# Gates of the side input taken tile by tile, and tokens kept in column order to the last store

## The chip, the cores and the metric

The kernel runs on one core of one Trainium2 chip. The metric is the device time of one execution in microseconds (us); lower is better. Engines are named as in the profile: PE (TensorE matmul), PEld (its weight loads), DVE (VectorE), ACT (ScalarE), POOL (GpSimd) and SP (SyncE). The transfers that SP and ACT issue are on their queues (SPq, ACTq).

## The reference, cut to what matters

Four layers over x of 512 tokens by 1024 features, all in float32: sparse attention (nsa), differential attention (diff), neighbourhood attention on a grid of 8 rows by 64 columns (na) and attention from latents with rotary positions (mla). The last two are each followed by a gated side input p ("ple"):

```python
for i in range(DEPTH):
    xn = rmsnorm_2(x, norm_g[i])
    y = mixer_na(...) if i % 2 == 0 else mixer_mla(...)   # ends in (o * silu(z)) @ w_out
    h = x + y
    gate = jax.nn.sigmoid(rmsnorm_2(h, ple_norm[i]) @ ple_w_gate[i])
    x = h + gate * (p[i] @ ple_w_proj[i])
return rmsnorm_2(x, final_norm)
```

In na a token (r, c) of the grid, number 64 r + c, attends to all 8 rows and a window of 16 columns. Every other operation of the second half is either by token or, in mla, over all tokens alike, except for the rotary tables, which depend on a token's position.

## The kernel before

**Numbers and tiles.** A product of two float32 matrices is made of three matmuls on parts: each operand is split into a high part of reduced precision and the rest (low), and low x high, high x low and high x high are summed in PSUM (`products`, L367 to L395; the matmul is L393). Tokens are 4 tiles of 128. A projection of 512 output columns ("block") over 1024 features is 8 chunks of 128, and its weights are two units of 1 MB, a=0 and a=1, each 128 x 2048 elements.

**Weights.** SP loads units in order (L308) into a ring of three slots. The unit n may be loaded once the unit before it in its slot is used up (`consumed`, L297): its last matmul for a=0 (`w_used`), or the last bank of the block for a=1 (`bank_done`). ACT then writes the high part (`split_high`, L339), POOL the low part by subtraction (`split_low`, L348, in one instruction or in quarters), and PE waits for `w_ready`. Each engine's order is written out by hand: all waits are on semaphores, and an engine that waits holds all that is behind it.

**Order of products.** `project_tensor` goes a=0 for the four tiles, then a=1 for the four tiles, so the four banks are done one after the other in the last quarter of the block. `project_by_tile` (L655) does a=0 and a=1 for one tile before it goes to the next, on block 1. `project_turning` (L641) takes an order of (a, tile, tile to turn): `TWO_TO_TURN` and `INTERLEAVED` (L638, L639).

**A norm chain.** Between two layers x (in SBUF) is squared tile by tile on ACT (`square_x`, L682), POOL takes the root (`root_x`, L733 and L735), DVE scales (`norm_tile`, L777), PE transposes the tile (`turn_tile`, L633, 8 transposes), ACT copies the high part (`high_tile`, L688) and DVE subtracts the low part (`low_tile`, L783). A tile's turn needs its norm, and for tiles 2 and 3 also the low part of the tile two before; the next layer's product for a tile needs that tile's low part.

**na and mla attention** (`pair_tensor`, `pair_vector`, `pair_scalar` L1310, `pair_pool` L1369). 32 steps for 16 groups of two steps (2 heads, 256 queries). A step: scores on PE, mask and maximum on DVE (L1267), exponent on ACT (L825), division on POOL (`normalise`, L1377), transposes on PE (L1197), high part on ACT (L1320), low part on DVE (L1280), values on PE (L1216). A group ends in a sum (ACT L1326, DVE L1287) and `gate_out` on POOL: times silu(z), which lies in the place of x (L1384), high part (L1390), low part (L1394). Before, na is computed in column order (8 c + r) and `by_token` writes its result back to token order with a stride of 64 elements. x itself lies in DRAM (`x_scratch`) during an attention: ACT stores it before, and fetches it after group 16 of the attention (`load_x`, L700, four transfers), before it fetches p (L1725). The out projection starts inside the attention (`first_output`); its second unit is split at the loop's end by ACT (step `steps + LAG - 1`) and by POOL (step `steps + LAG + 2`, ahead of the last `gate_out`).

**After the attention** the residual stage (`residual_*`) adds y to x (L601), and PE turns the normed tiles: tile 0 inside the last product of the out projection, tiles 1 to 3 inside the 8 products of the side input (`ple_tensor`, L1711). Then come the gates (`gate_tensor` L1799, `gate_scalar` L1804 with the sigmoid L1812, `gate_vector` L1843 with L1849 and L1852, `gate_pool` L1876), which add gate * side input to x. For ple0 the norm chain of mla runs at their end, with the first turn in the last product of the block; the other three turns are in `mla_cq`, by `INTERLEAVED`. Then follow `mla_ckv`, `mla_rope` (banks 0 and 1, taken by DVE at L1976 and L1977) and `mla_z`. For ple1 the final norm and the store (L328, one transfer per tile) end the program.

## Time and profile before

| | |
|---|---|
| median of 3 runs | 1449.52 us (1446.53 to 1450.22) |
| profiled execution | 1441.95 us, span 1440.1 us, granted clock 0.995 |
| PE / DVE / ACT / POOL busy | 1359.3 / 615.1 / 717.2 / 774.3 us |
| na attention | about 884 to 965 us of the span |
| na_out, side input, gates of ple0 | 965 to 1060 us |
| mla_cq, mla_ckv, mla_rope | 1060 to 1110 us |
| mla attention | about 1220 to 1335 us |
| mla_out, side input, gates of ple1, last norm | 1335 to 1440 us |

Times inside the span count from its start. A row of the timeline has the start, the duration, the engine, the line, what it writes and reads, the number of like instructions merged, and in brackets how long the engine sat idle before it and what released it. A matmul's duration is longer than the distance to the next one, since matmuls are pipelined: 186 of them fill 42.0 us, 0.226 us each.

### The profile page before, as it was taken

Reading aid. Unit: us, or ns where it says so; the run is one execution under the profiler, and the core shown is the slowest. Engines: PE = TensorE matmul, PEld = TensorE weight load, DVE = VectorE, ACT = ScalarE, POOL = GpSimd, SP = SyncE. Lnnn points to the kernel's source line nnn. Section 1 sums busy time; section 2 is a strip of 40 time slices with the busy share of each in tenths; the row PEclk is TensorE's granted clock in tenths of the full one; section 3 lists DMA queues with packets and bytes.
Section 4 is the critical chain, followed back from the end, with each engine's and each line's share of the span. In section 5 each row is a group of like instructions: output and inputs, shape, how many; then the busy total and the mean of one; then the engine's idle time right before and its main releaser. Section 6 shows DMA issues by size and latency. Waiting matters only on the chain.

```text
span 1440.1 us, 20940 instructions
## 1 busy us (share of the span) xinstructions
PE 1359.3 (94%) x7818; PEld 1113.8 (77%) x7818; DVE 615.1 (43%) x1606; ACT 717.2 (50%) x1533; POOL 774.3 (54%) x729
## 2 busy tenths in 40 slices
PE   5999999999999999889999999889999998999997
PEld 4887877777878888667788887678778886778785
DVE  3322068887330011883510014943242045887133
ACT  4244268887332323774423326954443254887252
POOL 5355256776444434486535334986446334566652
PEclk9999999999999999999999999999999999999998
DMA  6233210100453231213344224333234221001521
GB/s 243 88 118 117 89 59 31 31 30 12 151 176 117 88 110 67 74 46 122 119 140 146 88 89 146 118 112 138 103 115 163 88 91 56 1 2 67 182 88 59
DMA packets 27876, 139.57 MB, mean 97 GB/s; under 512 B 3328, under 2 KB 3712, under 8 KB 16128
## 3 DMA queue, kind: packets, MB, share of 16 engines
q1 hardware_dynamic: 14112, 98.57, 19.2%
q10 hardware_dynamic: 13664, 39.66, 8.1%
q8 instruction: 63, 1.03, 0.3%
q14 instruction: 37, 0.30, 0.1%
HBM read 129.83 MB, written 8.39 MB: 96 GB/s over the span
## 4 chain that ended last, share of the span: by engine, by line
PE 73%; POOL 10%; DVE 9%; ACT 4%; issue 2%; DMA 1%; ACTq 0%; POOLq 0%; SPq 0%; DVEq 0%
PE psum L393 59%; PE psum L1169 3%; POOL w_free L1377 3%; PE psum L1216 3%; PE psum L1197 3%; POOL w_lo L348 3%; DVE w_free L1267 2%; PE psum L908 2%; POOL split L1394 1%; DVE arena L777 1%; PE psum L1182 1%; ACT w_hi L339 1%; DVE u_lo L1280 1%; DMA w_raw<-in_weights 1%; POOL split L1390 1%
## 5 line engine op out<-in xcount | busy, mean ns | idle before, releaser
L348 POOL TENSOR_TENSOR w_lo<-w_raw,w_hi 128x2048 fp32r<-128x2048 f32 (+2 forms) x118 | 424.2, 3608 | 409.4 <-ACT w_hi L339 400.0
L393 PE MATMUL psum<-u_lo,w_hi 128*128 128x512 f32 (+1 forms) x712 | 279.8, 393 | 0.9 <-DVE arena L1976 0.9
L393 PE MATMUL psum<-u_hi,w_lo 128*128 128x512 f32 (+1 forms) x712 | 277.3, 389 | 0.0
L393 PE MATMUL psum<-u_hi,w_hi 128*128 128x512 f32 (+1 forms) x712 | 277.3, 389 | 0.0
L339 ACT ACTIVATE w_hi<-w_raw 128x2048 fp32r<-128x2048 f32 (+1 forms) x93 | 172.9, 1859 | 120.5 <-DMA w_raw<-in_weights 101.7
L393 PE MATMUL psum<-w_hi,split 128*128 128x512 f32 x608 | 195.6, 394 | 3.6 <-POOL w_lo L348 2.1
L825 ACT ACTIVATE w_free<-w_free,neg_max 128x256 f32<-128x256 f32 (+3 forms) x320 | 183.6, 580 | 12.4 <-DVE neg_max L947 7.3
L393 PEld LDWEIGHTS psum<-u_lo,w_hi 128*128 128x128 f32 (+1 forms) x712 | 133.2, 187 | 30.4 <-POOL w_lo L348 1.3
L393 PEld LDWEIGHTS psum<-u_hi,w_hi 128*128 128x128 f32 (+1 forms) x712 | 133.1, 187 | 28.6
L393 PEld LDWEIGHTS psum<-u_hi,w_lo 128*128 128x128 f32 (+1 forms) x712 | 133.2, 187 | 27.5
L393 PE MATMUL psum<-w_hi,u_lo 128*128 128x512 f32 (+2 forms) x352 | 133.8, 380 | 5.2 <-DVE u_lo L783 2.8
L1280 DVE TENSOR_TENSOR u_lo<-psum,u_hi 128x512 fp32r<-128x512 f32 (+3 forms) x256 | 124.8, 520 | 31.0 <-ACT u_hi L1320 27.7
L393 PEld LDWEIGHTS psum<-w_hi,split 128*128 128x128 f32 x608 | 114.2, 188 | 29.0 <-POOL w_lo L348 3.0
L1320 ACT ACTIVATE u_hi<-psum 128x512 fp32r<-128x512 f32 (+3 forms) x256 | 109.3, 463 | 49.0 <-PE psum L1197 45.5
L393 PE MATMUL psum<-w_lo,u_hi 128*128 128x512 f32 (+2 forms) x352 | 132.1, 375 | 0.0
L393 PE MATMUL psum<-w_hi,u_hi 128*128 128x512 f32 (+2 forms) x352 | 132.1, 375 | 0.0
L1197 PE MATMUL psum<-ident,w_free 128*128 128x128 f32 x704 | 111.8, 283 | 21.0 <-POOL w_free L1377 15.5
L393 PE MATMUL psum<-w_lo,split 128*128 128x512 f32 x304 | 118.4, 389 | 0.0
L1197 PEld LDWEIGHTS psum<-ident,w_free 128*128 128x128 f32 x704 | 75.9, 141 | 51.6 <-POOL w_free L1377 31.3
L1377 POOL TENSOR_SCALAR w_free<-w_free,inv 128x256 f32<-128x256 f32 (+1 forms) x128 | 73.2, 586 | 64.5 <-DVE inv L1273 64.2
L1216 PE MATMUL psum<-u_lo,split 128*128 128x256 f32 (+1 forms) x416 | 102.9, 284 | 0.0
L520 DVE SCALAR_TENSOR_TENSOR split<-psum,split 128x512 fp32r<-128x512 f32 x40 | 27.6, 692 | 171.2 <-ACT split L512 157.2
(193 smaller groups left out, 2157.1 us busy)
## 6 DMA issues: line engine op xcount, KB each, us to landing
w_raw<-in_weights SPq DMA_DIRECT2D x90, 1024.0 KB, 4.8
x<-x_scratch ACTq DMA_DIRECT2D x12, 512.0 KB, 6.1
gain<-in_gains ACTq DMA_DIRECT2D x10, 512.0 KB, 4.4
gain<-in_strips ACTq DMA_DIRECT2D x16, 256.0 KB, 2.9
spare<-in_strips ACTq DMA_DIRECT2D x16, 256.0 KB, 2.9
x_scratch<-x ACTq DMA_DIRECT2D x16, 256.0 KB, 5.1
gain<-in_near ACTq DMA_DIRECT2D x8, 512.0 KB, 4.2
w_raw<-in_near ACTq DMA_DIRECT2D x8, 512.0 KB, 3.7
```

Source lines behind the costliest of these rows:

```text
L339: high = nc.scalar.activation(w_hi[b][:, c], w_raw[b][:, c], ACT.Copy)
L348: low = nc.gpsimd.tensor_tensor(w_lo[b][:, c], w_raw[b][:, c], w_hi[b][:, c].bitcast(F32), ALU.subtract)
L393: mm = nc.tensor.matmul(dst, lhs, rhs, start=(a == 0 and k == 0 and (wl, ul) == (0, 1)), stop=(a + 1 == u and k + 1 == nk and (wl, ul) == ...
L825: nc.scalar.activation(p_map(f, i, m, n), p_map(f, i, m, n), ACT.Exp, scale=-1.0, bias=stat_of(neg_max, i, m), accum_out=stat_of(row_sum, ...
L908: mm = nc.tensor.matmul(head_bank(d, r), buf[:, pt:pt + P], split[:, a + v:a + v + P], start=(kt == 0 and nth == 0), stop=(kt == kts[-1] a ...
L1169: mm = nc.tensor.matmul(score_place(f, i, m), *products[m][nth], start=(nth == 0), stop=(nth == 2 and f is not mla_flow))
L1197: tr = nc.tensor.transpose(psum[:, 4 + m, kt * P:(kt + 1) * P], p_map(f, i, m, n)[:, kt * P:(kt + 1) * P], ident[:])
L1216: mm = nc.tensor.matmul(dst, value_place(f, d, m, kt), pt_pair(buf, d, m, a, b), start=(br == 0 and m == 0 and kt == order[0] and nth == 0 ...
L1267: nc.vector.tensor_tensor_reduce(out=p_map(f, i, m, n), in0=score_bank(i, m, n), in1=bias_of(f, i, m), scale=-1.0, scalar=BIG, op0=ALU.add ...
L1280: nc.vector.tensor_tensor(u_lo[:, c], bank(4 + m, n), u_hi[:, c].bitcast(F32), ALU.subtract).then_inc(f.low, 1)
L1320: nc.scalar.activation(u_hi[:, pt_cols(i, m, n)], bank(4 + m, n), ACT.Copy).then_inc(f.high, 1)
L1377: nc.gpsimd.tensor_scalar(p_map(f, i, m, n), p_map(f, i, m, n), stat_of(inv, i, m), factor_of(f, i, m), ALU.mult, ALU.mult).then_inc(f.p, 1)
```

## The change

- The gates' second block goes tile by tile (`project_by_tile`), with the turns of mla's tiles 0 and 1 inside tiles 2 and 3 of it; `mla_cq` has the other two (`TWO_TO_TURN`). ACT, DVE and POOL follow in a new order: the split of unit (1,1) of the gates comes earlier on ACT, those of `mla_cq` later on POOL and its second one later on ACT.
- The turns of the residual stage are all inside the side input's products, none in the out projection.
- `mla_rope` uses banks 4 and 5, and DVE gives the four banks of `mla_z` free in advance.
- From na on, x stays in column order: the store to `x_scratch` is four contiguous transfers in place of eight strided ones, `gate_out` writes without the large stride, p and the rotary tables are laid out in column order on the host, and the last store puts the rows in their place.
- x is fetched during the na and mla attentions, tile by tile (tiles 0, 1, 2 at ACT's steps 18, 26, 34), and only tile 3 after it.
- In na, ACT splits the out projection's second unit two steps earlier, and POOL does it in quarters after groups 12 and 13 in place of one instruction after group 14; the last `normalise` comes ahead of group 12.

```diff
@@ -325,7 +325,8 @@
                 sp.wait_ge(chain_normed, final_chain.n + t + 1)
-                sp.dma_start(out[t * P:(t + 1) * P, :], at(final_chain.xn + t * D, D)).then_inc(out_written, 16)
+                tile = bass.AP(out.tensor, 16 * t * D, [[D, 16], [GRID_W * D, 8], [1, D]])
+                sp.dma_start(tile, at(final_chain.xn + t * D, D)).then_inc(out_written, 16)
             sp.wait_ge(out_written, 16 * NT)
@@ -695,8 +696,8 @@
-        def load_x(act, source):
-            for t in range(NT):
+        def load_x(act, source, tiles=range(NT)):
+            for t in tiles:
                 act.dma_start(x[:, t * D:(t + 1) * D], source[t * P:(t + 1) * P]).then_inc(x_back, 16)
@@ -1342,29 +1343,27 @@
                     high(i - LAG)
-                if f in (na_flow, mla_flow) and i == f.steps + LAG - 1:
+                if i == (f.steps if f is na_flow else f.steps + LAG - 1) and f is not nsa_flow:
                     split_high(act, RUNS[f.name + "_out"]["unit"] + 1)
+                if f is not nsa_flow and i >= 18 and i % 8 == 2:
+                    t = (i - 18) // 8
+                    act.wait_ge(f.gated, 4 * t + 4)
+                    load_x(act, x_scratch, (t,))
                 j = i - LAG - 4 - 2 * (B - 1)
...
-        def by_token(part, u, h, n):
-            o = split[:, part + u * T:part + (u + 1) * T].rearrange("p (r c) -> p c r", r=8)
-            if h == 1:
-                return o[:, 24:56, :]
-            if n == 1:
-                return o[:, 8:24, :]
-            at_ = split[:, part + u * T:part + u * T + 1]
-            return bass.AP(at_.tensor, at_.offset, [at_.ap[0], [56, 2], [1, 8], [GRID_W, 8]])
+        def in_columns(part, u, h, n):
+            o = split[:, part + u * T:part + (u + 1) * T]
+            edge, _ = rotated(o)
+            return o[:, 192:448] if h == 1 else o[:, 64:192] if n == 1 else edge
...
             if g % 2 == 1:
-                return o.rearrange("p (c r) -> p c r", r=8)
-            if n == 1:
-                return o[:, P:2 * P].rearrange("p (c r) -> p c r", r=8)
-            return o[:, 0:P].rearrange("p (s c r) -> p s c r", s=2, c=8)
+                return o
+            return o[:, P:2 * P] if n == 1 else o[:, 0:P].rearrange("p (s c) -> p s c", s=2)
@@ -1395,13 +1394,18 @@
             for i in range(2, f.steps + LAG + 5):
-                if i - 2 < f.steps:
+                if i - 2 < f.steps - (1 if f is na_flow else 0):
                     normalise(i - 2)
-                if f in (na_flow, mla_flow) and i == f.steps + LAG + 2:
-                    split_low(pool, RUNS[f.name + "_out"]["unit"] + 1)
+                if f is na_flow and i == f.steps:
+                    normalise(f.steps - 1)
+                if f is mla_flow and i == f.steps + LAG + 2:
+                    split_low(pool, RUNS["mla_out"]["unit"] + 1)
                 j = i - LAG - 5 - 2 * (B - 1)
...
                     gate_out(j // (2 * B))
+                if f is na_flow and i in (f.steps, f.steps + 2):
+                    for part in range(i - f.steps, i - f.steps + 2):
+                        split_low(pool, RUNS["na_out"]["unit"] + 1, part)
@@ -1712,7 +1716,7 @@
             pe.wait_ge(p_lo, nth + 1)
-            turning = {(0, 0): 1, (0, 2): 2, (1, 0): 3}
+            turning = {(0, 0): 0, (0, 1): 1, (0, 3): 2, (1, 1): 3}
             for i in range(2):
@@ -1799,7 +1803,7 @@
             project_tensor(pe, name, only=(0,))
-            project_tensor(pe, name, only=(1,), between=chain and {(1, 1, 3): lambda: turn_tile(pe, chain, 0)})
+            project_by_tile(pe, name, None, {(0, 2): lambda: turn_tile(pe, chain, 0), (0, 3): lambda: turn_tile(pe, chain, 1)} if chain else {})
@@ -1812,32 +1816,29 @@
             split_next(act, name, 0, 0)
-            for j in range(NT):
+            take(0, 0)
+            split_next(act, name, 0, 1)
+            for j in range(1, NT):
                 take(0, j)
-            split_next(act, name, 0, 1)
+            take(1, 0)
             if c is final_chain:
-                take(1, 0)
-                take(1, 1)
                 square_x(act, c, 0)
-                take(1, 2)
-                square_x(act, c, 1)
-                take(1, 3)
-                square_x(act, c, 2)
-                square_x(act, c, 3)
+                for j in range(1, NT):
+                    take(1, j)
+                    square_x(act, c, j)
                 return
             split_next(act, name, 1, 0)
-            take(1, 0)
+            square_x(act, c, 0)
             take(1, 1)
-            square_x(act, c, 0)
+            high_tile(act, c, 0)
+            square_x(act, c, 1)
             take(1, 2)
-            square_x(act, c, 1)
-            high_tile(act, c, 0)
+            high_tile(act, c, 1)
+            square_x(act, c, 2)
             take(1, 3)
+            high_tile(act, c, 2)
+            square_x(act, c, 3)
             split_next(act, name, 1, 1)
-            square_x(act, c, 2)
-            high_tile(act, c, 1)
-            square_x(act, c, 3)
-            high_tile(act, c, 2)
             high_tile(act, c, 3)
@@ -1855,23 +1856,14 @@
             take(1, 0)
-            take(1, 1)
             norm_tile(dve, c, 0)
-            take(1, 2)
-            if c is final_chain:
-                norm_tile(dve, c, 1)
-                take(1, 3)
-                norm_tile(dve, c, 2)
-                norm_tile(dve, c, 3)
-                return
-            low_tile(dve, c, 0)
-            norm_tile(dve, c, 1)
-            take(1, 3)
-            low_tile(dve, c, 1)
-            norm_tile(dve, c, 2)
-            norm_tile(dve, c, 3)
-            low_tile(dve, c, 2)
-            low_tile(dve, c, 3)
+            for j in range(1, NT):
+                take(1, j)
+                if c is not final_chain:
+                    low_tile(dve, c, j - 1)
+                norm_tile(dve, c, j)
+            if c is not final_chain:
+                low_tile(dve, c, 3)
@@ -1882,16 +1874,17 @@
                 return
-            for part in range(4):
-                split_low(pool, n + 2, part)
             root_x(pool, c, 0)
+            pool.wait_ge(chain_normed, c.n + 1)
+            split_low(pool, n + 2, 0)
+            split_low(pool, n + 2, 1)
             root_x(pool, c, 1)
-            split_low(pool, n + 3, 0)
-            split_low(pool, n + 3, 1)
+            pool.wait_ge(chain_normed, c.n + 2)
+            split_low(pool, n + 2, 2)
+            split_low(pool, n + 2, 3)
             root_x(pool, c, 2)
             root_x(pool, c, 3)
-            split_low(pool, n + 3, 2)
-            split_low(pool, n + 3, 3)
+            split_low(pool, n + 3)
@@ -1969,15 +1962,13 @@
+            dve.wait_ge(bank_free["dve"], 4 + RUNS["mla_rope"]["taken"])
+            dve.sem_inc(bank_free["dve"], 4)
             dve.wait_ge(rope_in, 16)
-            def take(i, j):
-                if j == 0:
-                    return nc.vector.tensor_tensor(at(ROPE_TMP), bank(0), COS, ALU.mult)
-                return nc.vector.tensor_tensor(at(QT), bank(1), SIN, ALU.mult)
-            project_vector(dve, "mla_rope", take, banks=2)
-            run = RUNS["mla_rope"]
-            dve.wait_ge(bank_free["dve"], 4 + run["taken"] + 4)
+            dve.wait_ge(bank_done, 4 * RUNS["mla_rope"]["block"] + 4)
+            done("dve", nc.vector.tensor_tensor(at(ROPE_TMP), bank(4), COS, ALU.mult))
+            done("dve", nc.vector.tensor_tensor(at(QT), bank(5), SIN, ALU.mult))
+            settle("dve", dve)
             done("dve", nc.vector.tensor_tensor(at(QT), at(QT), at(ROPE_TMP), ALU.add))
@@ -2067,13 +2058,12 @@
             project_tensor(pe, "na_out", gated_by=na_flow, only=(0,), begun=True)
-            project_tensor(pe, "na_out", gated_by=na_flow, only=(1,),
-                           between={(1, 1, 3): lambda: turn_tile(pe, ple_chains[0], 0)})
+            project_tensor(pe, "na_out", gated_by=na_flow, only=(1,))
             ple_tensor(pe, ple_chains[0], 0)
             gate_tensor(pe, ple_chains[0], "ple0_gate", mla_chain)
-            project_turning(pe, mla_chain, "mla_cq", INTERLEAVED)
+            project_turning(pe, mla_chain, "mla_cq", TWO_TO_TURN)
             project_tensor(pe, "mla_ckv")
-            project_tensor(pe, "mla_rope", banks=2)
+            project_tensor(pe, "mla_rope", banks=2, base=4)
             project_tensor(pe, "mla_z", only=(0,))
@@ -2147,15 +2136,12 @@
             chain_scalar(act, na_chain, "diff_out", x_scratch)
-            for r in range(8):
-                column = x[r:P:8, :].rearrange("c (t d) -> c t d", t=NT)
-                act.dma_start(bass.AP(x_scratch.tensor, r * GRID_W * D, [[D, 16], [16 * D, NT], [1, D]]), column)\
-                    .then_inc(x_spilled, 16)
+            for t in range(NT):
+                act.dma_start(x_scratch[t * P:(t + 1) * P], x[:, t * D:(t + 1) * D]).then_inc(x_spilled, 16)
             project_scalar(act, "na_v", split_heads_act(by_head), halves=True)
...
             load_strips(act, na_flow, 0)
-            act.wait_ge(x_spilled, 2 * 16 * 8)
+            act.wait_ge(x_spilled, 16 * 8 + 16 * NT)
             project_scalar(act, "na_z", near_silu)
@@ -2276,10 +2262,15 @@
+def _column_order():
+    return np.arange(T) % 8 * GRID_W + np.arange(T) // 8
 def _constants():
...
     inv = (1.0 / (np.float32(10000.0) ** (np.arange(0, ROPE, 2, dtype=np.float32) / np.float32(ROPE)))).astype(np.float32)
-    ang = np.arange(T, dtype=np.float32)[None, :] * inv[:, None]
+    ang = _column_order().astype(np.float32)[None, :] * inv[:, None]
     cos, sin = np.cos(ang), np.sin(ang)
```

The other edits of the diff are the same in the mla half (no turn in `mla_out`, `load_x` of tile 3 alone), the counts of `x_spilled`, and p's layout on the host.

## Rows read from the trace of the kernel before

The timeline's columns are described above. Columns of the stretches: start and end, length, then busy time and number of instructions of each engine, granted clock of PE, share of the DMA engines and GB/s.

**Rows 1.** The page: the chain that ended last, by engine:
```profile
PE 73%; POOL 10%; DVE 9%; ACT 4%; issue 2%; DMA 1%; ACTq 0%; POOLq 0%; SPq 0%; DVEq 0%
```

**Rows 2.** Busy time by stretch: na attention; gates of ple0; mla_cq; mla attention:
```profile
900.96:944.63 43.67, 36.86 (x320) 30.08 (x320) 39.68 (x161) 39.99 (x131) 41.67 (x82) 1.00 0.28 98
1012.00:1054.00 42.00, 42.00 (x186) 34.72 (x186) 7.95 (x12) 13.95 (x15) 18.78 (x7) 1.00 0.32 113
1060.60:1085.70 25.10, 21.98 (x123) 20.91 (x124) 11.39 (x15) 9.48 (x13) 13.24 (x9) 0.93 0.51 189
1230.00:1310.00 80.00, 76.68 (x658) 59.45 (x657) 69.11 (x186) 65.66 (x151) 51.56 (x80) 1.00 0.01 2
```

**Rows 3.** Timeline of POOL in the na attention: an odd and an even group:
```profile
921.08 0.66 POOL L1390 TENSOR_SCALAR split<-spare 128x256 fp32r<-128x256 f32 x1
921.82 0.87 POOL L1394 TENSOR_TENSOR split<-spare,split 128x256 fp32r<-128x256 f32 x1
...
925.38 0.72 POOL L1390 TENSOR_SCALAR split<-spare 128x128 fp32r<-128x128 f32 x2
926.18 1.01 POOL L1394 TENSOR_TENSOR split<-spare,split 128x128 fp32r<-128x128 f32 x2
```

**Rows 4.** Timeline of POOL in the mla attention: one group:
```profile
1308.57 0.41 POOL L1390 TENSOR_SCALAR split<-gain 128x256 fp32r<-128x256 f32 x1
1309.06 0.73 POOL L1394 TENSOR_TENSOR split<-gain,split 128x256 fp32r<-128x256 f32 x1
```

**Rows 5.** ACT and PE at the end of the na attention; last row from the chain:
```profile
953.30 0.66 ACT L1320 ACTIVATE u_hi<-psum 128x256 fp32r<-128x256 f32 x2 [2.61 <-PE psum L1197]
...
966.38 0.50 PE L393 MATMUL psum<-w_hi,split 128*128 128x512 f32 x1 [1.52 <-POOL w_lo L348]
...
968.76 9.13 PE psum L393 x39
```

**Rows 6.** Low parts on POOL (timeline); high parts, loads of units (page):
```profile
1039.92 9.58 POOL L348 TENSOR_TENSOR w_lo<-w_raw,w_hi 128x2048 fp32r<-128x2048 f32 x5 [10.75 <-ACT w_hi L339]
...
L339 ACT ACTIVATE w_hi<-w_raw 128x2048 fp32r<-128x2048 f32 (+1 forms) x93 | 172.9, 1859 | 120.5 <-DMA w_raw<-in_weights 101.7
...
w_raw<-in_weights SPq DMA_DIRECT2D x90, 1024.0 KB, 4.8
```

**Rows 7.** Timelines of DVE and PE in mla_out, where x comes back:
```profile
1348.17 2.48 DVE L601 TENSOR_TENSOR x<-psum,x 128x512 f32<-128x512 f32 x4 [16.41 <-DMA x<-x_scratch]
...
1348.97 0.47 PE L393 MATMUL psum<-w_hi,split 128*128 128x512 f32 x1 [1.43 <-issue]
```

**Rows 8.** A turn, from the chain; PE in mla_cq, mla_ckv, ahead of mla_z:
```profile
998.59 0.87 PE psum L633 x8
...
1065.83 0.41 PE L393 MATMUL psum<-w_hi,u_lo 128*128 128x384 f32 x1 [1.91 <-DVE u_lo L783]
...
1070.48 0.52 PE L393 MATMUL psum<-w_hi,u_lo 128*128 128x384 f32 x1
...
1074.33 0.33 PE L393 MATMUL psum<-w_hi,u_hi 128*128 128x384 f32 x1
...
1092.54 0.39 PE L393 MATMUL psum<-w_hi,u_lo 128*128 128x256 f32 x1 [1.18 <-POOL w_lo L348]
...
1110.41 0.47 PE L393 MATMUL psum<-u_lo,w_hi 128*128 128x512 f32 x1 [0.94 <-DVE arena L1976]
```

**Rows 9.** Timelines of DVE and POOL beside each other, side input of ple0:
```profile
1006.78 3.59 DVE L777 SCALAR_TENSOR_TENSOR arena<-x,stat,gain 128x1024 f32<-128x1024 f32 x1
...
1004.67 4.61 POOL L348 TENSOR_TENSOR w_lo<-w_raw,w_hi 128x2048 fp32r<-128x2048 f32 x1
```

**Rows 10.** Chain in order of time, the last tiles of the kernel:
```profile
1430.70 1.29 DVE arena L777
...
1432.62 0.70 DVE x L1852
...
1435.83 1.29 DVE arena L777
```

13 lines of the change are left out of this document (6 added, 7 removed).

## The prediction

> **What bounds the kernel now.** I read the page first, for the chain of waits by engine [rows 1]: PE holds 73% of it, POOL 10%, DVE 9%, and transfers 1%. So time can be had only where PE stands still, or where the chain leaves PE. Next come the stretches [rows 2]. In the gates of ple0 PE is busy for all of 42.0 us; in the mla attention for 76.68 of 80. In the na attention it is busy for only 36.86 of 43.67 us while POOL has 41.67, ACT 39.99 and DVE 39.68: POOL sets the pace there, and the next two stand close behind it. In the 25.10 us of mla_cq PE is busy for 21.98, at a granted clock of 0.93. Then the timelines of the places that the diff touches, for the start times and the idle times in brackets.
>
> **1. na attention: writing in column order.** POOL's two instructions per group are the term. In an odd group, with the stride of 64 elements, the high part takes 0.66 and the low part 0.87 us [rows 3]; mla's group of the same size without the stride takes 0.41 and 0.73 [rows 4]. That is 0.39 us less. In an even group there are two pieces each (0.72 and 1.01 for the pairs, rows 3), and no row shows pieces of 128 without the stride: the saving is between 0 (all of it fixed cost) and the 0.39 of the whole piece; I take 0.2. A pair of groups has 43.67 / 5 = 8.73 us, so POOL alone would come to 8.73 - 0.59 = 8.14. But ACT's work in a pair is 39.99 / 5 = 8.0 and DVE's 7.9 [rows 2], and these three hand on to each other at every step, so I let the pair come to 8.33: 0.4 saved. POOL is the bound for about 5.5 pairs. Sum 2.2 us; bounds 0.5 (ACT takes over at once, three more transfers issued on its queue) and 5.5 x 0.73 = 4.0 (ACT's 8.0 is reached exactly). The waits of these fetches are on groups 4, 8 and 12 at ACT's steps 18, 26 and 34; POOL has done group 4t+4 in its step 14 + 8t, and ACT's high part of that same step needs a later division of POOL. They cost nothing.
>
> **2. End of the na attention.** PE stops at 964.7, is idle for 1.52 us until the low part of the second out unit, resumes at 966.38, has 9 matmuls (2.0 us at 0.226) and waits again, for the last group, until 968.76 [rows 5]. In the new order ACT writes the high part in its idle time of 2.61 us ahead of 953.30 [rows 5]: 1.9 us are needed [rows 6]. POOL took 9.58 us for a whole low part and four quarters of one [rows 6], so 4.8 for a unit; two quarters now stand in front of group 13 and two in front of group 14. All of them are done about 2.5 us before PE wants them, and the last group, which no longer stands behind the whole low part, ends near 966.2. PE then goes on at 964.7, and needs the last group at 964.7 + 2.05 = 966.75. 968.76 - 966.75 = 2.0 us. Without term 1's faster POOL it would be 1.4.
>
> **3. x is back sooner.** In mla_out DVE waits 16.41 us for x, and PE behind it 1.43 [rows 7]; the row says "issue", but PE resumes as the first of DVE's four adds (0.7 us each) ends. With three of four tiles there already, and p no longer behind them, that wait is gone; what is late next is PE itself. In na_out the same wait is barely there; 0.3 at most. Sum 1.7, bounds 1.3 and 1.9. The mla attention pays for three more issues on ACT, which is busy for 65.66 of 80 us [rows 2]: 0, bounds -0.5 and +0.5.
>
> **4. Gates by tile, mla_cq, mla_ckv, mla_rope.** A tile of the second block is now 24 matmuls, 5.4 us, so the norm chain of tile 0 starts 16 us before the block's end, not 8. PE has one more turn in the gates (0.87, rows 8) and one less in mla_cq. Now PE waits 1.91 us in mla_cq for a low part and 25.10 - 21.98 = 3.1 in all; it loses about 2 more through the clock, as matmuls that take 0.33 at the full level (2.4 GHz) take 0.52 after those waits, the level of 1.2 GHz [rows 8]. A replay from the rows: the gates end at 1060.9 (60.6 + the turn, less a wait that it replaces). mla_cq is 96 matmuls of 384 columns, 0.226 x 0.75 = 0.17 each by estimate, 16.5 us, and two turns, 1.7. Norm 2 and the low part of tile 3 come 0.6 late at best. At worst they come 2.2 late, and here is why: while POOL's low part ran from 1004.67 to 1009.28, DVE's norm, started at 1006.78, took 3.59 us in place of 1.29 and ended 1.1 after POOL's end [rows 9, 10]. POOL's quarters for mla_cq now lie beside the gates' products and sums on DVE (L1849, L1852). No row shows those two beside POOL: each may wait for nothing or for a quarter, 1.2 us. They read two operands of SBUF as the norm does, so I take the norm's row and the late end: mla_cq ends at 60.9 + 16.5 + 1.7 + 2.2 = 1081.3, for 1085.7. That is 4.4; with no such waits, 6.0. The Trainium skill has a rule for it that speaks against this order: in GPSIMD Engine Reference, Specifications, the two engines share their SBUF interfaces, and DVE instructions with two SBUF inputs contend. The norm's row agrees; by the rule the whole sum is 13.3 us, and without it 14.9.
> Its second unit is freed only in tile 3 of the gates, some 10 us later than now. Load 4.8, high part 1.9 [rows 6], low part 4.6 [rows 9]: 11.3 us, of which PE's last half tile and the first half of mla_cq cover about 13. No wait, but with 1 to 2 us to spare. mla_ckv's second unit is freed by the fourth of eight products, not the fifth: its 1.18 us go [rows 8]. mla_rope's unit is freed at the end of mla_cq and ready 11.3 us later, while mla_ckv gives 96 matmuls of half the columns, 0.113 each by estimate, 10.9: a new wait of 0.4. The 0.94 ahead of mla_z [rows 8], for the banks that DVE still reads, go with the other banks. Sum 4.4 + 1.2 - 0.4 + 0.9 = 6.1; bounds 3 (each of three units late by 1) and 7.7 (no contention, no new wait).
>
> **5. Residual stages.** The turns are the same 8 per half; tile 0's moves out of the out projection and ends about 3 us later against the rest. ACT's square of tile 3 and the high part behind it slip by the same, and DVE's norm 3 meets POOL's 4.6 us of the next unit as it does now [rows 9]. I take 0 twice; bounds +1 and -1.5 each.
>
> **6. Last tile.** After the last matmul DVE now does norm 1 first (to 1431.99), and only then the product and the sum of the last tile, which end at 1433.3; the last norm starts at 1435.83 [rows 10]. By tile, only tile 3 is left: its product can start 1.1 us sooner, and POOL's root no longer stands beside a norm, 0.2. 1.3 us; bounds 0.8 and 1.5. The store has rows of 4 KB as before: 0.
>
> Eight strided transfers to x_scratch become four, after diff_out; PE has no idle time there, so 0.
>
> **Sum.** 2.2 + 2.0 + 1.7 + 6.1 + 0 + 1.3 = 13.3 us. The profiled execution had 1441.95 us with a span of 1440.1, so it would come to 1428.7. The median of the runs shown is 7.6 above the profiled one; I take the difference off the median: 1449.5 - 13.3 = 1436.2.
>
> **Rivals.**
> A. *The weights become the bound.* By tile both units of a block are wanted within 2.7 us and freed late. For: the chain of load, high and low part is 11.3 us, and the spare above is 1 to 2 us, while ACT also issues the four stores of x there. Against: POOL is busy for only 13.24 of 25.10 us in mla_cq [rows 2]. Then term 4 keeps some 1 us, and the residual stages lose 1 each: 13.3 - 5.1 - 2 = 6.2, so 1443.
> B. *The faster POOL is hidden, and the quarters push the last groups.* ACT takes over in na, term 1 is 0.5 and term 2 1.0: 13.3 - 1.7 - 1.0 = 10.6, 1439. For: ACT's 39.99 against POOL's 41.67.
> C. *It doesn't do what it says.* x comes back no sooner, because its transfers wait on ACT behind the attention's own work, and the gates' norms are held by DVE and POOL: terms 3 and 4 fall to 0 and 2, 7.5 in all less 3 for both residual stages. 4.5, 1445, the edge of "the same".
> D. *Slower: the clock.* The new waits lie close together, in mla_cq and behind the moved turns. After such waits matmuls took 0.52 for 0.33 [rows 8], 0.15 us more from one to the next. To be slower by 4.35 us it must cost 17.7: some 120 matmuls at 1.2 GHz, all of mla_cq and half of mla_ckv. Now it was some 10. Price if it held for all of mla_cq and mla_ckv: 192 x 0.13 = 25 us: 1449.5 - 13.3 + 25 = 1461. Against: the clock fell behind idle times of PE, and the change leaves fewer of them.
>
> **How the numbers follow.** 0.3% of this kernel is 4.35 us, about what a measurement can tell from no change. Chances: forecast 0.66, B 0.13, A 0.11, C 0.07, D 0.03. The forecast's own range, from its bounds, is a gain of 9 to 18; with A and the lower part of B, and 2 us for medians that move, the range is 1430 to 1443. Faster: forecast, A, B and a third of C, 0.92, less 0.02 for what I don't see, 0.9. The same: 0.07. Slower: 0.03.
>
> **What the new profile would show.** Term 1: L1390 near 0.41 in na, and POOL's share in that stretch below ACT's. Term 2: no idle time of PE behind L348 at the end of na. Term 3: DVE's wait for x in mla_out below 8 us, and no idle PE there. Term 4: mla_z starts 6 us sooner against the start of the gates, and the clock stays at 1.00. Term 6: one norm behind the last matmul. The forecast would be wrong by: L1849 or L1852 above 2 us, or PE waiting for L348 in mla_cq or mla_rope by over 1 us.

## The result, and the profile after

| | before | after |
|---|---|---|
| median of 4 runs each | 1449.42 us (1446.53 to 1450.22) | 1432.17 us (1429.27 to 1433.38) |
| profiled execution | 1441.95 us, span 1440.1 | 1432.82 us, span 1431.0 |

The ratio is 0.9887, with an interval of 0.987 to 0.9905: faster by 13.8 to 18.8 us. The forecast of 1436.2 in 1430 to 1443 holds the time, and faster is the side on which it lay.

The two profiled executions differ by only 9.1 us, and that is misleading, as the last section shows: part of the kernel that the change doesn't touch ran at a lower granted clock in the second one. So I compare by stage. Five points of the program are easy to find in any of the traces: the start of the 155-us run of matmuls in na_v, the first sigmoid of ple0's gates, the start of a 56-us run of matmuls behind the latents of mla, the first sigmoid of ple1's gates, and the end. In the chain and in ACT's timeline of the changed kernel they are these:

```profile
724.82 155.30 PE psum L394 x684
...
1148.33 56.01 PE psum L394 x246
```

```profile
1030.06 0.60 ACT L1816 ACTIVATE arena<-psum 128x512 f32<-128x512 f32 x1 [3.23 <-PE psum L394]
...
1391.46 0.60 ACT L1816 ACTIVATE arena<-psum 128x512 f32<-128x512 f32 x1 [5.72 <-PE psum L394]
```

The stages between them, in us, each from one profiled execution:

| kernel | 1: to gates of ple0 | 2: to mla's long run | 3: to gates of ple1 | 4: to the end |
|---|---|---|---|---|
| before | 309.79 | 125.91 | 245.14 | 39.77 |
| after | 305.24 | 118.27 | 243.13 | 39.54 |
| gates alone | 309.35 | 118.38 | 245.05 | 38.43 |
| order of tokens alone | 305.30 | 126.54 | 243.39 | 41.10 |
| plain store | 305.20 | 118.49 | 243.09 | 38.44 |
| rows four apart | 305.14 | 119.59 | 243.09 | 38.42 |
| x fetched after | 306.00 | 118.41 | 245.38 | 39.59 |
| strided writes | 308.13 | 118.48 | 243.10 | 39.49 |
| late split | 306.68 | 118.72 | 243.12 | 39.54 |
| one turn | 305.24 | 135.34 | 243.11 | 39.52 |
| rope's banks | 305.11 | 119.82 | 243.18 | 39.57 |
| quarters | 305.14 | 119.10 | 243.20 | 39.52 |
| two queues | 305.16 | 119.42 | 243.12 | 43.58 |
| halves of features | 305.10 | 119.06 | 243.15 | 38.93 |

The change took 4.55, 7.64, 2.01 and 0.23 us, 14.4 in all. Where a kernel's code is that of the changed kernel in a stage, the stage repeats within 0.15 us, except for stage 2, which lies between 118.27 and 119.59. The section on stage 2 finds the one wait that makes this spread.

The page of the changed kernel, its chain by engine, beside [rows 1]:

```profile
PE 77%; DVE 9%; POOL 7%; ACT 4%; issue 2%; DMA 1%; ACTq 0%; POOLq 0%; SPq 0%; DVEq 0%
```

POOL went from 10% to 7% of the chain, and PE took it up. The stretches that answer to [rows 2] (five pairs of na groups, gates, mla_cq, mla attention):

```profile
902.30:944.70 42.40, 37.68 (x318) 30.09 (x318) 39.12 (x161) 40.05 (x131) 38.41 (x80) 1.00 0.42 148
1012.00:1054.00 42.00, 41.44 (x191) 34.55 (x192) 19.29 (x20) 18.08 (x22) 17.60 (x7) 1.00 0.24 88
1060.60:1085.70 25.10, 24.48 (x158) 23.75 (x157) 8.77 (x12) 9.45 (x10) 14.07 (x6) 1.00 0.71 270
1223.00:1303.00 80.00, 76.72 (x658) 59.53 (x658) 69.19 (x186) 65.87 (x152) 51.69 (x80) 1.00 0.05 15
```

Line by line: POOL, the busiest in na before, now has less to do there (38.41 us) than ACT (40.05) and DVE (39.12); in the stretch of the gates DVE is now busy for 19.29 us instead of 7.95, in part because some of its instructions take longer beside POOL; the stretch in which mla_cq lay has PE busy for 24.48 of 25.10 at a granted clock of 1.00; the mla attention is as it was.

### The profile page after: what moved, and what is told of

Read it like the earlier page. It is cut to its first block, busy times and chain, and to the rows that moved or that the text cites. A ratio compares the mean times of both kernels' runs of the same rounds, so it can differ in the third digit from the quotient of the medians.

```text
span 1431.0 us, 20938 instructions
## 1 busy us (share of the span) xinstructions
PE 1363.4 (95%) x7818; PEld 1118.5 (78%) x7818; DVE 625.5 (44%) x1606; ACT 717.5 (50%) x1533; POOL 766.8 (54%) x729
## 4 chain that ended last, share of the span: by engine, by line
PE 77%; DVE 9%; POOL 7%; ACT 4%; issue 2%; DMA 1%; ACTq 0%; POOLq 0%; SPq 0%; DVEq 0%
PE psum L394 61%; PE psum L1170 3%; PE psum L1198 3%; PE psum L1217 3%; DVE w_free L1268 2%; POOL w_free L1376 2%; PE psum L909 2%; POOL w_lo L349 2%; PE psum L1183 1%; DVE u_lo L1281 1%; DVE arena L778 1%; ACT w_free L826 1%; POOL split L1393 1%; PE psum L1648 1%; PE psum L634 1%
```

## The experiments

All are edits of the changed kernel, but for the first, which edits the kernel before. (The line numbers of some kernels differ by one or a few.)

### Each half alone

Gates alone: the kernel before with the new gates, turns, `mla_cq` order and rope banks. Order alone: the changed kernel with those four undone.

```diff
 # order alone
-            project_by_tile(pe, name, None, {(0, 2): lambda: turn_tile(pe, chain, 0), (0, 3): lambda: turn_tile(pe, chain, 1)} if chain else {})
+            project_tensor(pe, name, only=(1,), between=chain and {(1, 1, 3): lambda: turn_tile(pe, chain, 0)})
-            project_turning(pe, mla_chain, "mla_cq", TWO_TO_TURN)
-            project_tensor(pe, "mla_rope", banks=2, base=4)
+            project_turning(pe, mla_chain, "mla_cq", INTERLEAVED)
+            project_tensor(pe, "mla_rope", banks=2)
```

> The kernel before with the gates' half of the change alone: gates by tile, turns moved, mla_cq in the new order, rotary part on banks 4 and 5; x fetched after the attention, token order and plain store as before. My theory: the stretch from the start of ple0's gates to mla_z is 7.5 to 8 us shorter than before, the last tile's tail (last matmul to end) 1.3 us shorter since its store lands in 2.6 us, the rest unchanged: 9 us faster, 1440. Rival: that half needs x to be back early (PE is behind x in both out projections) and gives 5 us or less; then the waits in mla_cq come back.

> The changed kernel with the gates' half undone: column order, x fetched during the attentions, the earlier split at the end of na, and the store in column order. My theory: na attention 1.9 us shorter, the stretch to na_out's second block 2.3 shorter, mla_out's 1.4 to 1.7 shorter, the store's landing 1.1 us longer: 4.8 us faster than before, 1444.5. Rival: the two halves overlap, and this one alone gives 8 or more.

Gates alone: 1438.08 us, ratio 0.9935 (0.9912 to 0.9959). Order alone: 1444.73, ratio 0.998 (0.9961 to 0.9999). By stage the gates gave 0.44, 7.53, 0.09 and 1.34, the order 4.49, -0.63, 1.75 and -1.33. So stage 2 is the gates' work alone, stages 1 and 3 are the order's but for 0.4 and 0.1, and in stage 4 the two work against each other: the gates save 1.3 and the order costs 1.3. Both came as expected (9.4 us by stages for 9, and 4.3 for 4.8), and neither rival did. The -0.63 of the order in stage 2 is no work of its own: PE waits 1.83 us for the second unit of mla_ckv in that trace, and waited 1.18 in the trace of before.

### Stage 4: the last store

```diff
 # plain store
-                tile = bass.AP(out.tensor, 16 * t * D, [[D, 16], [GRID_W * D, 8], [1, D]])
-                sp.dma_start(tile, at(final_chain.xn + t * D, D)).then_inc(out_written, 16)
+                sp.dma_start(out[t * P:(t + 1) * P, :], at(final_chain.xn + t * D, D)).then_inc(out_written, 16)
 # rows four apart
+                tile = bass.AP(out.tensor, t * D, [[4 * D, P], [1, D]])
```

> The changed kernel with its four stores contiguous in DRAM (rows stay in column order, so they land in other places of the output). My theory: the last tile's store lands in 2.6 us, not 3.7, the issue takes 0.34 us, not 0.54, and the stretch from the last matmul to the end is 8.4 us, not 9.7: 1.2 us faster than the changed kernel. Rival: the store is slower for when it runs, not for its layout: no change.

> The changed kernel with its last stores scattered less far: a row of the output still takes one 4 KB piece, but neighbouring rows of a tile go four rows (16 KB) apart instead of 64 rows (256 KB) apart, so the values land at other rows of the output. The issue and the packets stay as they are. In the changed kernel such a store lands in 3.7 us and its issue takes 538 to 656 ns; with the 128 rows side by side (plain store) it was 2.6 us and 332 to 348 ns. Theory D (distance): what costs is that pieces written at the same time lie 256 KB apart; at 16 KB apart the store lands within 0.3 us of 2.6, and the stretch from the first sigmoid of the last gates to the end is near 38.5 us. Theory N (neighbours): any gap between the rows costs it, since side by side the 128 pieces are one run of memory; then it lands in 3.5 to 3.9 us and the stretch stays near 39.5 us. The issue time tells the same of the descriptor's shape: two dimensions here and three in the changed kernel, so an issue near 340 ns would put that part down to the third dimension.

Plain store: 1431.68 us, ratio 0.9891 (0.9858 to 0.9924), which can't be told from the changed kernel's; stage 4 is 38.44, 1.10 shorter. Rows four apart: one execution, 1432.24; stage 4 is 38.42. The store by its line and tile, first in the changed kernel (durations of the issue, then the time to landing):

```profile
L329 SPq DMA_DIRECT2D out_x<-arena x4: 538/543/656, 1410.7 to 1426.9; - x4
...
DMA to landing us min/median/max: 3.7/3.7/3.8
```

with the plain store:

```profile
L328 SPq DMA_DIRECT2D out_x<-arena x4: 332/338/348, 1409.4 to 1425.6; - x4
...
DMA to landing us min/median/max: 2.6/2.6/2.6
```

and with the rows four apart:

```profile
L329 SPq DMA_DIRECT2D out_x<-arena x4: 332/338/348, 1411.2 to 1427.4; - x4
...
DMA to landing us min/median/max: 2.6/2.6/2.6
```

Each is 128 pieces of 4 KB. That neighbouring rows don't touch costs nothing: 16 KB apart they land in 2.6 us as side by side. It is the form of the changed kernel, three dimensions with 256 KB between neighbours, that costs 1.1 us. Which of the two it is, the third dimension or the distance, these runs don't tell apart; the issue is longer with it too (543 for 338 ns). The busy share of the 16 DMA engines (in tenths) and the rates in the DMA view, over a window of the changed kernel (1415 to 1431 us) and of rows four apart (1418 to 1431), in 40 slices each, show where the time is:

```profile
DMA  0000049979500000000999791000000039988700
GB/s 0 0 0 0 0 113 225 174 154 440 205 0 0 0 0 0 0 0 0 236 195 164 256 420 41 0 0 0 0 0 0 0 82 236 184 164 358 287 0 0
```

```profile
DMA  9900000000000029997000000000000499950000
GB/s 403 416 13 0 0 0 0 0 0 0 0 0 0 0 88 403 416 403 303 0 0 0 0 0 0 0 0 0 0 0 0 189 403 403 403 214 0 0 0 0
```

The changed kernel's stores run at some 150 to 250 GB/s for most of their time and come near 400 only at their end; the others are at 403 from the start. In the middle of a store the DMA engines are busy for 70% or more in both, so in the changed kernel they take longer over a piece; they don't stand idle for want of pieces.

Two attempts to win it back: the store of each tile in two halves of its partitions, the second on ACT's queue, and the last tile's norm and store in two halves of the features.

```diff
 # two queues
+                act.dma_start(tile, at(final_chain.xn + t * D, D, 64, P)).then_inc(out_written, 16)
 # halves of features, last tile: norm of 512 features, store of 512, twice
+                    tile = bass.AP(out.tensor, 16 * t * D + h * D // 2, [[D, 16], [GRID_W * D, 8], [1, D // 2]])
```

> The changed kernel, with each tile's last store as two transfers of 64 rows, one issued by SP and one by ACT. My theory: the store in column order is slow at its destination (packets of the same size move at some 160 GB/s in its middle, against 420 with contiguous rows), so two queues with the same rows land no sooner than 3.4 us and the span is within 0.4 us of the changed kernel. Rival: it is slow in the issue and the making of descriptors (0.54 us for 0.34), which halves with two queues: 1 us faster.

> The changed kernel, with the last tile's norm and store in two halves of 512 features. My theory: the first half's transfer runs beside the second half's norm, the stretch from the last matmul to the end gets 0.4 to 0.8 us shorter. Rival: rows of 2 KB instead of 4 make the same number of packets twice, and the end is later by 0.3 or more.

Two queues: 1435.37, ratio 0.992 (0.9895 to 0.9946), and stage 4 is 4.0 us longer, where the theory had it within 0.4 us and the rival 1 us shorter. ACT's transfers stand behind all of its sigmoids and squares, as its timeline shows; the last line is the busy share of the DMA engines from 1418 to 1432 us:

```profile
1420.33 1.19 ACTq L2190 DMA_DIRECT2D out_x<-arena  x1
...
1421.56 3.08 ACTq L2190 DMA_DIRECT2D out_x<-arena  x3
...
DMA  0000354344255445454555434253464342220000
```

All four of ACT's halves are issued within 4 us at the end, so the experiment piled transfers up. It also changed a second thing: with transfers of 64 rows no slice has the DMA engines busy for 70%, where those of 128 rows reach 90% or more. So it says nothing about the split of a tile by itself. Halves of features: 1432.69, ratio 0.9894 (0.9864 to 0.9924), the same as the changed kernel's within what can be measured; by stage 0.61 us shorter, in the 0.4 to 0.8 that were expected. A half lands in 2.8 to 2.9 us.

### Stage 1 and stage 3: when x is fetched

```diff
-                if f is not nsa_flow and i >= 18 and i % 8 == 2:
-                    t = (i - 18) // 8
-                    act.wait_ge(f.gated, 4 * t + 4)
-                    load_x(act, x_scratch, (t,))
...
-            load_x(act, x_scratch, (NT - 1,))
+            load_x(act, x_scratch)
```

> The changed kernel with x fetched after the attentions, as before. My theory: PE waits again for the first add of x, 1.4 us in mla_out and, because PE now gets there 2 us sooner, up to 2 us in na_out; nothing else moves: 3 us slower than the changed kernel. Rival: the fetches cost the attentions as much as they give (ACT issues three more transfers in each), so the time is the same within 1 us.

1435.71 us, ratio 0.9928 (0.9907 to 0.9949). Stage 1 is 0.76 longer than after and stage 3 by 2.25, 3.0 in all as expected. In na_out PE is idle for 0.62 us that the changed kernel doesn't have. PE and DVE in mla_out, first of this kernel:

```profile
1341.89 2.48 DVE L602 TENSOR_TENSOR x<-psum,x 128x512 f32<-128x512 f32 x4 [16.95 <-DMA x<-x_scratch]
...
1342.68 0.47 PE L394 MATMUL psum<-w_hi,split 128*128 128x512 f32 x1 [2.00 <-issue]
```

then DVE of the changed kernel:

```profile
1336.94 1.89 DVE L602 TENSOR_TENSOR x<-psum,x 128x512 f32<-128x512 f32 x3 [12.12 <-DMA x<-x_scratch]
1340.66 0.69 DVE L602 TENSOR_TENSOR x<-psum,x 128x512 f32<-128x512 f32 x1 [1.83 <-PE psum L394]
```

The 2.00 us of PE "issue" are in the one and not in the other, where PE has no idle time between 1329.39 and 1373.98. DVE still waits 12.12 us for x: its wait is for all four tiles (one count on `x_back`), and the fourth is still fetched after the attention. But it resumes early enough that PE finds a free bank.

### Stage 1: the stride, and the end of the na attention

Strided writes: `in_columns` is replaced by `by_token` of the kernel before, and `o_part` likewise. Late split: the second out unit is split by ACT and POOL in the steps of the kernel before.

```diff
 # late split, POOL
-                if f is na_flow and i in (f.steps, f.steps + 2):
-                    for part in range(i - f.steps, i - f.steps + 2):
-                        split_low(pool, RUNS["na_out"]["unit"] + 1, part)
+                if f in (na_flow, mla_flow) and i == f.steps + LAG + 2:
+                    split_low(pool, RUNS[f.name + "_out"]["unit"] + 1)
```

> The changed kernel, but the na groups are written with the stride of 64 elements again (values land in other places). My theory: this is term 1 alone: a pair of groups takes 8.7 us again, not 8.49, and the stretch from na_v to the first sigmoid of ple0's gates grows from 305.2 us by 1.5 to 2.5. Rival: ACT sets the pace of the na attention by now, and it grows by less than 0.5.

> The changed kernel, but the second unit of na's out projection is split late, as before. My theory: PE is idle for some 1.5 us on POOL's low part and waits for the last group, and the stretch from na_v to the first sigmoid grows from 305.2 us by 2.0. Rival: with x back early, the delay is taken up by PE's later waits, and it grows by less than 0.7.

One execution each: 1437.25 and 1431.1, and stage 1 is 2.89 and 1.44 us longer than after, for 1.5 to 2.5 and 2.0 expected. POOL in the na attention of the changed kernel, beside [rows 3] and [rows 4]:

```profile
917.12 0.41 POOL L1389 TENSOR_SCALAR split<-spare 128x256 fp32r<-128x256 f32 x1
917.61 0.74 POOL L1393 TENSOR_TENSOR split<-spare,split 128x256 fp32r<-128x256 f32 x1
...
921.41 0.57 POOL L1389 TENSOR_SCALAR split<-spare 128x128 fp32r<-128x128 f32 x2
922.06 0.88 POOL L1393 TENSOR_TENSOR split<-spare,split 128x128 fp32r<-128x128 f32 x2
```

An odd group saves 0.38 us (0.25 + 0.13) and an even one 0.28 (0.15 + 0.13). PE's waits in the na attention, two to a pair, and at its end, with strided writes:

```profile
925.76 0.90 PE L1198 MATMUL psum<-ident,w_free 128*128 128x128 f32 x4 [0.81 <-POOL w_free L1382]
930.01 0.89 PE L1198 MATMUL psum<-ident,w_free 128*128 128x128 f32 x4 [0.55 <-POOL w_free L1382]
934.59 0.90 PE L1198 MATMUL psum<-ident,w_free 128*128 128x128 f32 x4 [0.88 <-POOL w_free L1382]
...
974.34 0.50 PE L394 MATMUL psum<-w_hi,split 128*128 128x512 f32 x1 [0.42 <-POOL split L1399]
```

and without them, in the changed kernel:

```profile
923.46 0.90 PE L1198 MATMUL psum<-ident,w_free 128*128 128x128 f32 x4 [0.63 <-POOL w_free L1376]
927.32 0.89 PE L1198 MATMUL psum<-ident,w_free 128*128 128x128 f32 x4 [0.15 <-POOL w_free L1376]
931.99 0.90 PE L1198 MATMUL psum<-ident,w_free 128*128 128x128 f32 x4 [0.61 <-POOL w_free L1376]
```

A pair takes 8.8 us with the stride (934.59 - 925.76) and 8.5 without (931.99 - 923.46). (The first number of a row is where PE resumes.) The stride also costs at the end of the attention, where PE then waits 0.42 for the last group; in the changed kernel PE runs without an idle time from 962.78 to 1002.3, through the whole end of the attention. With the late split it waits there again, for the unit's low part:

```profile
965.87 0.50 PE L394 MATMUL psum<-w_hi,split 128*128 128x512 f32 x1 [1.22 <-POOL w_lo L349]
```

### Stage 2: order, banks, and DVE beside POOL

One turn: in the gates only tile 0 is turned, and mla_cq has the old order. Rope's banks: banks 0 and 1 again. Quarters: the low part that lies beside the gates' first products on DVE is made in four instructions.

```diff
 # one turn
-  {(0, 2): lambda: turn_tile(pe, chain, 0), (0, 3): lambda: turn_tile(pe, chain, 1)}
+  {(0, 3): lambda: turn_tile(pe, chain, 0)}
-            project_turning(pe, mla_chain, "mla_cq", TWO_TO_TURN)
+            project_turning(pe, mla_chain, "mla_cq", INTERLEAVED)
 # quarters
-            split_low(pool, n + 1)
+            for part in range(4):
+                split_low(pool, n + 1, part)
```

> The changed kernel, with gates by tile, but only tile 0 of mla's norm chain turned in them and mla_cq in the old order, with three turns. My theory: it is the norm chain ending early that gives the gain, and the order of mla_cq decides when mla_ckv's second unit is freed: PE waits for a low part of the weights again, 1 to 2 us, and the turns fall closer together: the stretch from the first sigmoid to the long run of mla_z grows from 118.3 us by 1.5 to 3. Rival: the order doesn't matter once the gates go by tile: below 0.5.

> The changed kernel with the rotary part on banks 0 and 1 again. My theory: PE waits for DVE ahead of mla_z, 0.94 us as before, and the stretch from the first sigmoid to the long run of mla_z grows from 118.3 us by 0.9. Rival: the wait was taken up elsewhere: no change.

> The changed kernel, with POOL's low part of the gates' last unit in quarters, so that DVE's product (L1850), which took 4.73 us beside the whole one, gets in between. My theory: the product takes 1.9 us at most, and the time does not change by over 0.3, since DVE's sums of the first block have 5 us to spare. Rival: the held DVE delays the norm chain, and the stretch from the first sigmoid to mla_z gets 0.5 us or more shorter.

**One turn**: one execution, 1450.72 us, beside 1443.78 for one execution of the kernel before on the same chip; stage 2 is 17.1 us longer than after, for 1.5 to 3 expected, and the whole gain of the change is gone. PE in mla_cq, and ACT between them:

```profile
1065.07 0.44 PE L394 MATMUL psum<-w_hi,u_lo 128*128 128x384 f32 x1 [3.36 <-POOL w_lo L349]
...
1067.56 0.60 ACT L689 ACTIVATE u_hi<-psum 128x512 fp32r<-128x512 f32 x1 [7.73 <-PE psum L634]
...
1081.89 0.69 PE L394 MATMUL psum<-w_hi,u_lo 128*128 128x384 f32 x1 [7.36 <-POOL w_lo L349]
```

and PE's stretch from 1055 to 1105 us:

```profile
1055.00:1105.00 50.00, 36.59 (x203) 33.91 (x202) 14.96 (x19) 16.20 (x20) 19.82 (x12) 0.90 0.39 140
```

Only PE went back to its old order here; ACT and POOL kept the new one, and that is what the run measures. ACT copies the high part of tile 1 ahead of the sigmoid of tile 3's gates (L1816), and PE now turns tile 1 only in mla_cq: ACT is idle for 7.73 us, and the gates, squares and norms behind it are late. POOL writes half of the first unit's low part only behind the norm of tile 1: 3.36 us. The old order wants the second unit for its third product, ahead of the last turn, but its high part stands on ACT behind the high part of tile 2, and its low part on POOL behind the roots of all four tiles: 7.36 us. The order of the turns and the order of the copies and splits are one decision. The granted clock was 0.90 in this stretch.

**Rope's banks**: one execution, 1430.5. The idle time of 0.94 us ahead of mla_z [rows 8] is back, though the trace puts it down to a low part:

```profile
1101.16 0.47 PE L394 MATMUL psum<-u_lo,w_hi 128*128 128x512 f32 x1 [0.94 <-POOL w_lo L349]
```

The low part that ended then is that of mla_z's second unit, which is wanted only half a block later. DVE's first product of the rotary part ended at 1101.01, 0.15 us before PE resumed, as in the kernel before (1110.26 and 1110.41). Stage 2 is 119.82; with the moving wait below taken off, it is 1.2 us longer than in the changed kernel, so the theory (0.9) holds and the rival doesn't.

**Quarters**: one execution, 1430.14; stage 2 is 119.10, within the spread. DVE's first products of block 0 of the gates, in the changed kernel with the low part in one instruction beside it on POOL:

```profile
1034.57 4.73 DVE L1850 TENSOR_TENSOR arena<-arena 128x512 f32<-128x512 f32 x1 [2.46 <-ACT arena L1816]
...
1034.13 4.62 POOL L349 TENSOR_TENSOR w_lo<-w_raw,w_hi 128x2048 fp32r<-128x2048 f32 x1 [3.93 <-ACT w_hi L340]
```

and in quarters:

```profile
1031.01 1.40 DVE L1850 TENSOR_TENSOR arena<-arena 128x512 f32<-128x512 f32 x1 [2.49 <-ACT arena L1816]
1032.45 1.67 DVE L1853 TENSOR_TENSOR x<-x,arena 128x512 f32<-128x512 f32 x1
1034.04 1.78 DVE L1850 TENSOR_TENSOR arena<-arena 128x512 f32<-128x512 f32 x1
```

An instruction of 0.69 us takes 4.73 and ends 0.55 after POOL's; beside quarters it takes 1.4 to 1.8. This is the rule of the Trainium skill (GPSIMD Engine Reference, Specifications) that two SBUF inputs on DVE contend with POOL, and the trace agrees. But the time doesn't move: behind the long product DVE is idle again for 1.68 us before the next block's first product, and with the moving wait taken off, stage 2 is 118.27 us here too.

**The moving wait.** Where the 1.3 us of stage 2's spread lie is seen in the chain of this kernel, behind mla_cq:

```profile
1069.28 8.20 DMA w_raw<-in_weights
1077.50 1.92 ACT w_hi L340
1079.49 4.62 POOL w_lo L349
1084.15 50.93 PE psum L394 x246
```

In words: the load of a unit, its high part, its low part, and then PE's matmuls. The unit is the second of mla_ckv, the one that PE waited 1.18 us for before [rows 8]. PE is idle for 0.83 us ahead of it here, for 1.16 with two queues, for 1.32 with rows four apart, and for nothing that shows in the changed kernel's own trace, where the low part was done at 1086.79 and PE went on at 1086.84. The code there is the same in all of them: PE has caught up with the load of a unit (8.20 us here, a median of 4.8 over the kernel) and its two splits. With this wait taken off, stage 2 is 118.24 to 118.30 us in nine kernels: the changed one and all its edits but order alone, one turn and rope's banks.

## Why the prediction was right, and where it wasn't

**Term 1, the stride (2.2): right, at 2.9.** The size per pair was too hopeful (0.4 foreseen, 0.25 to 0.3 measured), and the last groups gave more than I had counted. That ACT, busy for 40.05 of 42.4 us, is the next limit fits the busy times, but no run takes work off it, and PE still waits for POOL (0.15 and 0.6 us).

**Term 2, the end of na (2.0): right, at 1.4** with term 1 in place. The idle time behind the low part is gone. The forecast let the faster POOL's share of 0.6 at this place stand in term 2; the runs put it into term 1. The two terms were 4.2 together, and the two costs add up to 4.3.

**Term 3, x back sooner (1.7): right in kind, too small in size, at 0.8 + 2.25 = 3.0**, above its bound of 1.9. I took the price of the wait from PE's 1.43 us "issue" in the kernel before [rows 7] and 0.3 for na_out. With all else changed those idle times are 2.00 and 0.62. The test "DVE's wait below 8 us" failed (12.12): I had thought three tiles would free three adds, and the wait is for all four.
Terms 1 to 3 taken singly make 7.3, and the stages gave 4.55 + 2.01 = 6.6: nearly 0.8 is counted more than once.

**Term 4, the gates by tile and mla_cq (6.1): right in kind, at 7.6**, near the upper bound of 7.7. (That bound still holds the new wait of 0.4; without contention and without that wait the terms give 8.1.) Some of it is luck: the moving wait, which the forecast had going for good, was 0 in this trace, and up to 1.32 in others of the same code, so against the same trace of before other executions gain 6.3 to 7.6. PE's idle times were 5.4 us before (1.91, 1.18 and 0.94 [rows 8], and 0.64, 0.49 and 0.27 in the same trace), of which 0.62 is left: 4.8. The rest of the stage went from 120.48 to 117.65. By estimate the granted clock gave 0.07 x 25.1 = 1.8 of that 2.8 (0.93 to 1.00 in the stretch of mla_cq), and the banks of the rotary part 0.3 (117.91 with the old ones); some 0.8 I can't place.

Two steps missed. The first is the replay's late end, norm 2 and the low part 2.2 us late: mla_ckv starts 56.17 us behind the first sigmoid before and 50.91 after, 5.3 sooner and not 4.4. The contention came as the norm's row had it, but I carried its whole length through to PE. In the changed kernel the add of tile 2 took 1.66 us for 0.69, and tile 2's square, root and norm came later by it; but PE turned tile 2 without a wait. Tile 3's chain starts anew with its own sigmoid, for which DVE waited 0.19 us, and none of its instructions was lengthened. Its low part kept PE waiting for 0.62. The second is the new wait of 0.4 ahead of mla_rope, which didn't come: the unit was ready 11.6 us behind the end of mla_cq (1092.58 and 1080.97), and PE shows no idle time there. The rows of the first:

```profile
1056.53 3.38 POOL L349 TENSOR_TENSOR w_lo<-w_raw,w_hi 128x512 fp32r<-128x512 f32 x2 [1.40 <-DVE arena L778]
...
1057.09 1.66 DVE L1853 TENSOR_TENSOR x<-x,arena 128x512 f32<-128x512 f32 x1
...
1062.41 0.69 DVE L1850 TENSOR_TENSOR arena<-arena 128x512 f32<-128x512 f32 x1 [0.19 <-ACT arena L1816]
...
1069.06 1.29 DVE L784 TENSOR_TENSOR u_lo<-psum,u_hi 128x512 fp32r<-128x512 f32 x2 [1.38 <-ACT u_hi L689]
...
1070.49 0.41 PE L394 MATMUL psum<-w_hi,u_lo 128*128 128x384 f32 x1 [0.62 <-DVE u_lo L784]
```

The sign by which the prediction would call itself wrong, L1849 or L1852 above 2 us, did appear (4.73), with no cost behind it: it was a bad sign, for it named a duration and not a wait of PE.

**Term 5, residual stages (0): right.** Stage 3 of gates alone gained 0.09.

**Term 6, the last tile (1.3 and 0 for the store): the total was wrong.** The by-tile order gave 1.34, as forecast. "The store has rows of 4 KB as before: 0" is the step that failed: it costs 1.1 with the gates and 1.3 without, so 0.2 was left. I had priced the store by bytes and pieces and had bounded nothing, though no row that I had read showed that shape.

**The sum.** 14.4 by stages for 13.3 forecast. By stage the forecast had 4.5, 6.1, 1.4 and 1.3: it was off by 0.05, 1.5, 0.6 and -1.1, and a part of that cancelled. The median moved by 17.3, with an interval of 13.8 to 18.8, which holds the 14.4. The forecast of 1436.2 was 4.0 above the measured 1432.17: the stages are 1.1 of that, and what the other 2.9 are isn't shown; they are of the size by which the granted clock of untouched stages moves a time.

**The rivals.** *A, the weights:* its mechanism is there, but small: a wait of 0 to 1.32 us ahead of mla_ckv's second unit. In one turn, where ACT's and POOL's order no longer fits PE's, the waits for low parts took 12 us. *B, the faster POOL hidden:* no; 2.9 us came of it. *C:* no. *D, the clock:* no; it rose to 1.00 in the changed places. One turn shows D's mechanism where the waits are long (0.90). (D's 120 matmuls are mla_cq and a quarter of mla_ckv, not half.)

## What to carry to other kernels

When the order of products on PE is changed so that a tile ends earlier, move the splits and turns of the next layer in the same edit: here the same new gates are worth 7.6 us when all engines' orders fit, and lose 9.4 when PE alone keeps its old order behind them (125.91 to 135.34). Price a lengthened instruction by the idle time that stands behind it before the next engine that waits, not by its own length. And a layout that is carried to the end of a kernel is paid for in the last store, the one transfer that nothing covers: look at its landing time by itself.

## What the runs showed of the hardware that I had not expected

- **The shape of a store's target.** 512 KB in 128 pieces of 4 KB land in 2.6 us side by side or 16 KB apart, and in 3.7 us as 16 x 8 pieces with 256 KB between neighbours. Which of the two, shape or distance, costs the 1.1 us isn't shown.
- **The granted clock of an untouched stage differs from run to run.** The windows from 580 to 680 us, in the differential attention, whose code is the same in all these kernels: before, changed, and order alone.

```profile
580.00:680.00 100.00, 88.11 (x619) 69.63 (x618) 71.41 (x259) 67.81 (x254) 65.75 (x118) 1.00 0.23 74
```

```profile
580.00:680.00 100.00, 89.30 (x600) 70.56 (x599) 72.06 (x259) 67.28 (x253) 61.00 (x117) 0.93 0.18 63
```

```profile
580.00:680.00 100.00, 90.19 (x577) 71.86 (x576) 73.51 (x262) 65.28 (x248) 57.95 (x111) 0.86 0.16 54
```

At 1.00, 0.93 and 0.86 the na_v run starts at 719.49, 724.82 and 731.47 us. Other kernels whose clock was 1.00 there start it at about 721, those at 0.93 at 724.0 to 726.2. So a difference of some 10 us between two profiled executions can arise before the first changed instruction. The 7.6 us between the median and the profiled run of before may be of this kind: in other runs of the kernel before, 1444.18 us went with a mean clock of 0.995 and 1449.48 with 0.988. Where in those runs the time went isn't shown. What sets the clock there these runs don't show.
- **A binding wait that moves by itself.** The wait for mla_ckv's second unit was 0 to 1.32 us in executions of the same code, and the load in front of it took 7.5 to 8.7 us where it was in the chain.
